# Pass counts by step kind, cached rows requested by GpSimd, and a planned layer-1 projection in a two-layer streaming encoder kernel

## The reference

```python
def mixer_ab(h, pos, w_in, f_bias, w_out, cache):      # layer 0
    qa, ka, va, fa, ga, qb, kb, vb, iq, ik, iw, gb = split_cols(h @ w_in, AB_COLS)
    ...
    qb = apply_rope(qb.reshape(b, t, H_B, DH_B), pos)
    kb = apply_rope(kb.reshape(b, t, H_B, DH_B), pos)
...
def dsa_block(q, iq, iw, qpos, kv, ik, kpos, n_sel):
    score = jnp.einsum('bqh,bqhk->bqk', iw.astype(jnp.float32), rel)
    _, sel = lax.top_k(score, n_sel)
...
def mla_block(q_lat, q_rope, qpos, ckv, krope, kpos):  # layer 1
    s = (jnp.einsum('bqhc,bkc->bhqk', q_lat, ckv)
         + jnp.einsum('bqhr,bkr->bhqk', q_rope, krope)).astype(jnp.float32) * ((NOPE + ROPE_DIM) ** -0.5)
```

## Time and profile before

| | us |
|---|---|
| median of 3 runs | 1914.26 (1907.79 to 1914.31) |
| profiled execution | 1914.62 |
| its span | 1912.9 |
| PE busy | 1681.3 |
| DVE busy | 1292.8 |
| ACT busy | 941.6 |
| POOL busy | 222.4 |

### The profile page before, as it was taken

How to read it: one execution, slowest core, us unless ns; L and a number is a source line. 1 busy time by engine, 2 the same in 40 slices (tenths; PEclk the granted TensorE clock), 3 DMA queues, 4 the chain that set the end, 5 groups by cost and what they waited for, 6 DMA issues and landing times. The chain is left out here.

```text
span 1912.9 us, 34157 instructions
## 1 busy us (share of the span) xinstructions
PE 1681.3 (88%) x12683; PEld 1316.9 (69%) x12754; DVE 1292.8 (68%) x2800; ACT 941.6 (49%) x1884; POOL 222.4 (12%) x305
## 2 busy tenths in 40 slices
PE   5895889999989957899997989798986998999798
PEld 2563568888767836677776878577774776667687
DVE  3543767879999925678887645554275777777764
ACT  4313542228111455678885226356735667767421
POOL 2301000001001012101100000100005222221000
PEclk9995989999999978999998999899997999999899
DMA  9776213422134039987764633242234111111432
GB/s 334 217 245 141 70 50 100 133 93 94 28 101 135 34 91 242 228 206 199 198 191 154 247 147 101 78 112 94 79 75 106 28 37 36 28 36 43 155 132 99
DMA packets 228685, 235.17 MB, mean 123 GB/s; under 512 B 139301, under 2 KB 163397, under 8 KB 226474
## 3 DMA queue, kind: packets, MB, share of 16 engines
q1 hardware_dynamic: 221770, 213.07, 39.1%
q0 software_dynamic: 6752, 19.92, 2.9%
HBM read 173.98 MB, written 58.95 MB: 122 GB/s over the span
## 5 line engine op out<-in xcount | busy, mean ns | idle before, releaser
L528 PE MATMUL PS<-ab_wh,hT 128*128 128x512 f32 x576 | 231.8, 402 | 5.8 <-DVE ab_wl L870 5.8
L529 PE MATMUL PS<-ab_wl,hT 128*128 128x512 f32 x576 | 227.2, 394 | 0.0
L530 PE MATMUL PS<-ab_wh,hT 128*128 128x512 f32 x576 | 226.7, 394 | 0.0
L1361 DVE TENSOR_SCALAR_CACHE_REDUCE topk_junk<-scores,topk_small 128x528 bf16<-128x528 f32 (+6 forms) x224 | 194.5, 915 | 1.3
L2538 DVE CUSTOM_DVE_ANT_0 la_S<-PS,la_mask 128x128 f32<-128x128 f32 (+3 forms) x144 | 107.6, 747 | 41.7 <-PE PS L530 28.5
L528 PEld LDWEIGHTS PS<-ab_wh,hT 128*128 128x128 f32 x576 | 109.6, 190 | 29.0 <-ACT ab_wh L798 4.0
L530 PEld LDWEIGHTS PS<-ab_wh,hT 128*128 128x128 f32 x576 | 109.4, 190 | 25.4
L1711 ACT ACTIVATE at_P<-at_S,at_nm 128x128 f32<-128x128 f32 (+2 forms) x144 | 110.5, 767 | 30.2 <-DVE at_nm L1756 30.0
L529 PEld LDWEIGHTS PS<-ab_wl,hT 128*128 128x128 f32 x576 | 109.3, 190 | 22.3
L528 PE MATMUL PS<-out_wh,out_mT 128*128 128x512 f32 x288 | 115.9, 402 | 4.7 <-DVE out_mT L2014 4.7
L2460 ACT ACTIVATE la_P<-la_S,la_nm 128x128 f32<-128x128 f32 (+3 forms) x144 | 110.4, 766 | 9.3 <-DVE la_nm L2538 9.1
(11 more groups left out here) (431 smaller groups left out, 4445.8 us busy)
## 6 DMA issues: line engine op xcount, KB each, us to landing
ab_wl_raw<-in_ab_w_in SPq DMA_DIRECT2D x64, 256.0 KB, 4.8
out_g<-scratch_gates_nat SPq DMA_DIRECT2D x18, 512.0 KB, 5.5
hT_raw<-in_ada_w SPq DMA_DIRECT2D x8, 1024.0 KB, 15.6
mod_w<-in_ada_w SPq DMA_DIRECT2D x16, 512.0 KB, 6.5
mod_w<-in_ada_w SPq DMA_DIRECT2D x8, 1024.0 KB, 6.5
at_kc<-in_cache_a_k SPq DMA_DIRECT2D x8, 1024.0 KB, 12.9
at_vc<-in_cache_a_v SPq DMA_DIRECT2D x8, 1024.0 KB, 10.0
at_kc<-in_cache_b_k SPq DMA_DIRECT2D x8, 1024.0 KB, 7.8
```

Source lines behind the costliest of these rows:

```text
L528: nc.tensor.matmul(out, x[0], w[0], start=start, stop=False)
L529: nc.tensor.matmul(out, x[0], w[1], start=False, stop=False)
L530: return nc.tensor.matmul(out, x[1], w[0], start=False, stop=stop)
L1361: go(V.tensor_scalar(mark, x, limit, 0.0, op, ALU.add, accum_out=cnt[:, m:m + 1]), 0 if m == M - 1 else 1)
```

## The change

Three parts. First, `idle` runs by the kind of the group a step belongs to: 5 passes in a copy step, 4 in a silu step, 1 in a rope step, and in the last step all that are left. Second, in the attention of layer 0 the four loads of a batch are issued by GpSimd in `load_batch`, with the same waits; batch 0 at the stage's start, batch g + 1 behind the split of head g + 1's values. Third, the krope group is gone. A class `KeyRope` loads its 32 weight columns at the start of the layer-1 projection and multiplies one span of three tiles in each of steps 9, 12 and 15, turns, rotates and splits its three tiles together in the two steps behind, and stores them; `LatentPlan` gives the order of steps, loads and splits: latent, queries 0, then gate 0 and queries 1 in turns, five steps of queries 2, then gate 1 with the 13 other query steps between. Gates take the weight slot of the latent group, queries slots 1 and 2. A query step waits for its own tile of the query latent, not for all nine.

```diff
-def projection(nc, c, name, groups, idle=None, pair=BF16, ring=4, front=None, weights=None):
+def projection(nc, c, name, groups, idle=None, pair=BF16, ring=4, front=None, weights=None, plan=None, narrow=None):
...
-    steps = [(g, i) for g in range(len(groups)) for i in range(NT)]
+    steps = plan.steps if plan else [(g, i) for g in range(len(groups)) for i in range(NT)]
...
             if before_in_slot(g) is not None:
-                sp.wait_ge(mm_done, NT * (before_in_slot(g) + 1))
+                sp.wait_ge(mm_done, last_step[before_in_slot(g)] + 1)
...
-                    if groups[g].kind == "qc" and g == min(q for q in range(len(groups)) if groups[q].kind == "qc") and i == 0:
-                        pe.wait_ge(kept_lo, NT)
+                    if groups[g].kind == "qc":
+                        pe.wait_ge(kept_lo, i + 1)
...
+class KeyRope:
...
+        self.at = lambda q: NT + 3 * q
...
+    def pe(self, pe, s):
+        nc, PS, ident = self.nc, self.c.PS, self.c.ident
+        q = self.span(s, 0)
+        if q is not None:
+            pe.wait_ge(self.w_lo, 1)
+            self.front.wait_tile(pe, NT - 1)
+            if q:
+                pe.wait_ge(self.T_lo, q)
+            for k in range(KT):
+                last = product(nc, PS[0:RD, 6, 0:SPAN], [self.wh[:, k, :], self.wl[:, k, :]],
+                               [t[:, k, q * SPAN:(q + 1) * SPAN] for t in self.hT], k == 0, k == KT - 1)
+            last.then_inc(self.mm_done, 1)
+        q = self.span(s, 1)
+        if q is not None:
+            pe.wait_ge(self.across_read, q + 1)
+            if q:
+                pe.wait_ge(self.row_done, q)
...
+        q = self.span(s, 2)
+        if q is not None:
+            pe.wait_ge(self.row_done, q + 1)
...
+class LatentPlan:
...
+        behind = [q2[5:6], q2[6:8], q2[8:9], q3[0:2], q3[2:4], q3[4:6], q3[6:7], q3[7:9], []]
+        self.steps = [(self.LATENT, i) for i in range(NT)] + [(self.Q0, i) for i in range(NT)]
+        for gate, query in zip(g0, q1):
+            self.steps += [gate, query]
+        self.steps += q2[0:5]
+        for gate, queries in zip(g1, behind):
+            self.steps += [gate] + queries
...
+        self.split_steps |= {a + 2 + k: [(self.Q2, k)] for k in range(3)} | {b - 4 + k: [(self.G1, 2 * k), (self.G1, 2 * k + 1)] for k in range(4)}
...
+PASSES = {"copy": 5, "silu": 4, "rope": 1}
...
-        for _ in range(-(-topk.passes() // (n - 2)) if s < n - 1 else topk.passes()):
+        for _ in range(PASSES[groups[s // NT].kind] if s < n - 1 else topk.passes()):
...
+            def load_batch(l):
+                x, h = l // H, l % H
+                if l >= 2:
+                    pool.wait_ge(turned, number["keys", l - 2, NP - 1] + 1)
+                pool.dma_start(kc[:, l % 2], cache_k[x][0, h].rearrange("(j p) h d -> p j (h d)", p=P)).then_inc(kc_in[l % 2], 16)
+                if l >= 2:
+                    pool.wait_ge(maxed, batch_at(l - 2) + 1)
...
             for g in range(G):
                 if g + 1 < G:
                     split_v(g + 1)
...
-                if g < H:
-                    pool.wait_ge(add_in[g % 2], 16 * (g // 2 + 1))
-                    nc.gpsimd.tensor_tensor(addt[:, g % 2, PAST:], addt[:, g % 2, PAST:], c.new_tri[:], ALU.add).then_inc(causal, 1)
+                if g + 1 < G:
+                    load_batch(g + 1)
+                    causal_new(g + 1)
```

More of the change, by code:

```diff
@@ L679, in projection @@
     keep = lambda g: groups[g].keep
[L680 to L683, removed]
-    steps = [(g, i) for g in range(len(groups)) for i in range(NT)]
+    steps = plan.steps if plan else [(g, i) for g in range(len(groups)) for i in range(NT)]
+    last_step = [max(s for s, (q, i) in enumerate(steps) if q == g) for g in range(len(groups))]
     turned = [s for s, (g, i) in enumerate(steps) if groups[g].turned]
@@ L734, in _ @@
                 load_weights(sp, 0)
+            if narrow:
+                narrow.load(sp)
             if front:
@@ L853, in _ @@
                         nc.scalar.activation(hi, src[:, 0:hi.shape[1]], ACT.Copy).then_inc(kept_hi, 1)
-                if s < len(steps) and steps[s][0] + 1 < len(groups):
-                    for k in split_steps.get(steps[s], []):
-                        split_high(steps[s][0] + 1, k)
+                for g, k in split_steps.get(s, []):
+                    split_high(g, k)
+                if narrow:
+                    narrow.act(act, s)
         @block.vector
@@ L927, in _ @@
                                                    op0=ALU.mult, op1=ALU.subtract).then_inc(T_lo, 1)
[L928 to L933 removed]
+                for g, k in split_steps.get(s, []):
+                    split_low(g, k)
+                if narrow:
+                    narrow.dve(dve, chain, s)
+                if idle and s < len(steps):
+                    idle(dve, s, len(steps))
         @block.tensor
         def _(pe):
[L937 to L948 removed]
             if front:
@@ L1409, in steps, with selection @@
             yield
-def selection(nc, c):
+PASSES = {"copy": 5, "silu": 4, "rope": 1}
+def selection(nc, c, groups):
     tiles = [(QT, TOPK_S)] + [(i, TOPK_P) for i in SELECT_TILES]
@@ L2089, in queries @@
             turned = lambda i: [c.s["qcT"][d, 4 * g:4 * g + 4, :, i * P:(i + 1) * P].rearrange("h p t -> p h t") for d in range(2)]
[L2090 to L2091 removed]
+            return Group(cq, QL // P, w_q, n * g, n, "qc", None, turned, C_SCALE, slot=1 + g % 2)
+        narrow = KeyRope(nc, c, front, hT, QL + KVL, stack)
+        projection(nc, c, "c", [latent, queries(0), queries(1), gate[0], queries(2), gate[1], queries(3)], front=front, plan=LatentPlan(), narrow=narrow)
 def latent_attention(nc, c, front, out):
@@ L2666, in build @@
                 c.topk.small = inner.enter_context(nc.sbuf_tensor("topk_small", [P, 9, len(SELECT_TILES) + 1], F32))
-                projection(nc, c, "ab", groups, selection(nc, c), weights=weights)
+                projection(nc, c, "ab", groups, selection(nc, c, groups), weights=weights)
             retire_semaphores(nc)
```

209 lines of the change are left out of this document (136 added, 73 removed).

## The result

The changed kernel takes 1878.69 us in the median of 4 runs (1876.75 to 1879.56), the kernel before 1914.28 in the runs beside it; the ratio is 0.9828, with an interval of 0.9804 to 0.9852. The profiled execution took 1879.56, with a span of 1877.8. The forecast was 1880, from 1862 to 1900.

A forecast was written before the change was run, and what follows sets the result against it. PE, busy for 88% of the span, bounds the kernel, so only its standing time or lower clock can shrink. -14 + 0 - 21 = -35 from 1914.62 gave 1879.6, called 1880 us; range for 8 in 10: 1862 to 1900.

The forecast's parts named there:

- Part A: Layer-0 projection, selection passes moved out of the rope steps so that PE sets their pace: -14 us, from -9 to -15.
- two steps of slack and two steps without passes behind them: 0: Last group of the layer-0 projection: the longer final passes leave DVE some 4 us late, which costs nothing.
- Part B: Layer-0 attention, cached rows requested by GpSimd in place of SP: 0 us, from -14 to +16.
- 3 before PE's first product: Head 0 of layer-0 attention: of 4.4 us for the early first keys, 3 fall before PE's first product.
- +4 for the later heads: Layer-0 attention from head 1 on: each load waits for more, keys come just in time; +4 us, bounds +20 and -10.
- waits without a semaphore: Layer-0 attention: PE's waits that name no semaphore, gone if the queue is less pressed; counted in the bound of -10 us.
- Rival (4): Layer-0 attention gives more, waits without semaphore gone and no later ones come: -12 us, 1868; chance 0.15.
- Rival (1): Layer-0 attention: GpSimd's chain sets the heads, slower; 1911 at 24 us per head, 1927 at 26; chances 0.08 mild, 0.04 strong.
- Part C: Layer-1 projection, narrow products and their rotation moved inside the first query group: -21 us, from -14 to -26.
- query group with the rotary keys: Layer-1 projection: nine query steps, narrow products, small transposes and span waits of 1 us each, 37.6 us in all.
- nine pairs: Layer-1 projection: nine pairs of gate and query step, paced by PE, 69.3 us.
- last product to the next request: End of the layer-1 projection: ACT's chain, the last gate, its landing and 0.5 us to the next stage, 8.6 us.

## Why the forecast was right, point by point

**Part A**, forecast -14, from -9 to -15: measured -11.1. Up to the last product it gave 15.7, 10.2 of it waits of PE (10.1 in the forecast). PE became the bound in the rope groups, and the copy groups with five passes cost nothing, at 52.28 of 53.60. The step that failed is the last one, "two steps of slack and two steps without passes behind them: 0". The slack holds for PE, which indeed did not wait; but the stage ends with the stored gate row, and for that row there is no slack. It cost 4.6 us.

**Part B**, forecast 0, from -14 to +16: measured -7.5, alone -8.2. At the start, "3 before PE's first product" was 8.4, and the head came out 2.6 shorter, not 4.4. The step that failed is the +4 for the later heads. It rested on 12.9 us for the keys to land and on DMA engines that could give no more. The landing was 12.9 in that trace alone, 9.1 to 9.3 in the three others where SP requests full batches and 6.9 to 8.8 in the nine with GpSimd, and in the changed kernel PE waited for keys once, 2.4 us in head 1, and not in a later head. The waits without a semaphore, which the forecast let stand only in its lower bound, were what moved: 15.2 to 5.4 us. Rival (4) is the nearest to this part's course.

Rival (1), the slower one, did not come: GpSimd's request took 0.8 and not more beside a DVE busy for 104.0 of 133.7 us. The Trainium skill's trap (SBUF — State Buffer, "The 'DVE blocks DMA' trap (SWDGE)") is about DVE copies from SBUF to SBUF. In these heads all of DVE's large groups read PSUM (`at_PT<-PS`, `at_S<-PS`, `at_kT<-PS`, `mix<-PS`), so no run here tests it.

The Trainium skill's rule that several initiating engines save only the sequencer's time (DMA: Bandwidth & Descriptors, "Issuing engines are not separate DMA queues") is not refuted by these runs, but what it calls usually small was not: SP's requests over heads 1 to 7 took 78.8 us before and 34.6 after. The forecast drew from it that B is no more than a reordering and put B at 0; the early order gave 0.9994 on SP and 0.9948 with GpSimd's requests.

**Part C**, forecast -21 for the stage (and 1 late at its start): measured -13.5, just outside -14 to -26. The terms, from the trace, forecast first: query group with the rotary keys 37.6 and 45.0; nine pairs 69.3 and 68.6; five query steps 16.5 and 13.7; gate and query steps 77.7 and 79.5; last product to the next request 8.6 and 11.45. Two terms failed. In the query group I counted the spans' waits at 1 us each by engines, and did not follow SP's queue, where moved loads stood ahead of stores: 3.2 to 4.8 of the 7.4 us are shown to be that. In the tail I took 0.5 from landing to the next stage, as the kernel before has it (1443.59 to 1444.06, behind a store of SP); behind the landing of GpSimd's gate row it is 3.15, of which its DRAIN is 2.58.

The sum was right in good part by luck: these misses, +2.9, -7.5 and +8, cancel to within 4 us, and the opening stage was 3.9 shorter in the profiled run by chance. The range of each part was of more use than its value: two of three held.

## What to carry to other kernels

A moved step moves its requests too: follow each queue past which it goes, the stores of other steps included. Slack of the bound engine is not slack of the stage's end: look what the last stored row waits for. A transfer's landing time belongs to its neighbours and differs even between kernels with the same order, so don't carry one median over when the queue changes. And an engine that closes a stage with a slow last instruction sets the stage's end as soon as its own last store is late.

## What the runs showed of the hardware

PE's waits without a semaphore, over heads 1 to 7, are 10.7 to 15.8 us in four traces where SP requests the cached rows, 4.0 to 9.7 in nine where GpSimd does, and 2.2 where a quarter of those bytes is loaded. All 51 over 0.4 us end 1.2 to 2.0 us behind the landing of a 16 KB packet of the instruction queue.

A request of 1 MB by GpSimd occupies it for 0.77 to 0.82 us, one of 264 KB for 0.65, one of 32 KB for 0.54 to 0.55, in the changed kernel. A request of 1 MB by SP took 0.36 us at the least and 6.11 at the most in the kernel before.

GpSimd's DRAIN at the end of a block took 4.45 to 4.46 us behind the layer-0 projection and 2.58 to 2.99 behind the layer-1 projection, in all 14 traces, SP's 0.01 to 0.14 in the kernel before and the changed one. In all nine kernels with the new plan the next stage's first request came 3.15 to 3.16 us after the last gate row's landing (in the changed one 1405.45 to 1408.60); in the five with the old order it came 0.47 us after SP's last landing. In the layer-0 projection the last gate row lands at 684.01 in the changed kernel and q is requested at 689.50: most of these 5.5 us is the DRAIN too, before as after.
